# Deferred-norm FFN: one matmul of 512 columns for two of 256, with the sums of the parts taken on ScalarE and VectorE

## The chip, the core and the metric

The kernel runs on one core of a Trainium2 chip. The metric is the device time of one execution in microseconds (us); three runs of the kernel before give 2852.6 to 2856.93, median 2855.45.

## The reference

Two blocks of layers are computed one after the other on x of 256 tokens by 1,024 features. What matters here is the second block, which has four layers. Each does a mixer (differential attention, a gated linear recurrence, or a chunked gating unit), a cross attention to a memory, and then this FFN:

```python
def rmsnorm(x, g):
    y = xf * lax.rsqrt(jnp.mean(xf * xf, axis=-1, keepdims=True) + EPS)
    ...
def swiglu(h, w_gu, w_down):
    gate, up = jnp.split(h @ w_gu, 2, axis=-1)
    return (jax.nn.silu(gate) * up) @ w_down
...
        x = x + swiglu(rmsnorm(x, norm_ffn[i]), ffn_w_gu[i], ffn_w_down[i])
```

The inner width is 2,816. The first block has two layers with two FFNs each, with the same width, whose norm carries a modulation.

## The kernel before

**Precision.** Every large product is made from two parts: a value v is split into hi (v rounded to fp32r) and lo (v - hi), and three of the four products of parts are summed: weights hi x hi, weights hi x lo, weights lo x hi. The helper `product` (L1889 to L1891) issues these as three matmuls of 256 columns (the 256 tokens), each with a weight load of its own.

**Weights.** They stream from HBM through four slots in a fixed order. SyncE (queue SP) loads a unit into `raw`; ScalarE (ACT) rounds it to `whi` (L767); VectorE (DVE) forms `wlo` (L1187); TensorE (PE) uses both and signals `used`. A slot holds one unit, so its next split waits for `used`. The splits are issued by `ahead(pos)`, which stands between the other instructions of ACT and DVE and runs at most three units ahead. Both engines work in order, so a split waits behind whatever stands ahead of it.

**The FFN.** It has 11 steps of 256 inner features. Step n has a unit A (gate columns), a unit B (up columns) and two units O0, O1 (rows of the output weights). PE's order is A(0), B(0), then A(n+1), B(n+1), outs(n) for n from 0 to 9, and outs(10). A and B have each 16 groups (k, m): 8 tiles k of the features by two halves m of the 256 inner features. A is summed in the PSUM bank of its slot, both halves m in one bank; so is B. outs(n) has 48 matmuls (L2058; the last outs is L2091) into banks 4 to 7, from `ghi` and `glo`, the two parts of the product silu(A) x B.

**The deferred norm.** In the four FFNs of the second block (`st.defer` is set) x is not yet normalized when A and B are computed: `fhi`, `flo` (the halves of `parts_f`) are the parts of x times the gain, and the root of the norm, `rstd`, is multiplied in behind the matmuls. PE sums the squares (L2011) between A(0) and B(0); ACT takes Ln (L826) and Exp (L828) of that; DVE multiplies A by the root (L1381), ACT takes Silu (L853), DVE multiplies by the root again (L1384) and by B (L1389), ACT rounds to `ghi` (L866), DVE forms `glo` (L1393). In step 0 the split of A(1) stands behind Silu on ACT, and the split of B(1) behind `ghi`, which waits for the product. The FFNs of the first block go another way through the same functions (L858, L1400, L1403) and are not touched.

Of the kernel before, what the change touches and what calls it, by code (L numbers as in the profile page):

```python
# [29 lines left out]
P = 128  # L30
D = 1024
KT = D // P
# [202 lines left out]
def build(nc, a, out):  # L235

    ctx = ExitStack()
    with ctx:
# [51 lines left out]
        def work(at, *dims):  # L290
# [64 lines left out]
            "const_in const_rest mem_in token_in rows_first rows_in misc_in bias_out aux_in "  # L355
            "rows_turned misc_turned bias_mm vec_copied tok_turned tok_copied pro_v pro_s c_ready "
            "ada_sum ada_red ada_col "
            "ffn_out ffn_silu ffn_sr norm_sq norm_add norm_ss norm_ln norm_rs norm_gain norm_t norm_hi norm_lo "
            "ffn_hi ffn_lo ffn_scale x_new "
            "gn_sq gn_ss gn_ln gn_rs gn_out rope_mm rope_cos rope_done "  # L360
            "gate_mm gate_s gate_v taps_v conv_mm conv_v conv_s conv_hi conv_lo "
# [200 lines left out]
        def tiles4(v, cols, keep=slice(None)):  # L562
            return v.rearrange("p (c t) -> p c t", t=cols)[:, keep, :]

        def ffn_pos(st, j):

            base = st.pos + 2 + 4 * (j - 1)
            return (st.pos, st.pos + 1, None, None) if j == 0 else (base, base + 1, base + 2, base + 3)
# [11 lines left out]
        def summed(u):  # L580

            return 8 * (u if isinstance(u, int) and u <= ADA_BY_PE[0] else u - ADA_BY_PE[1] + ADA_BY_PE[0])

        SG_V = SG_T = 4
        MIX_F = (0, 20)

# [19 lines left out]
        def rows2(v):  # L606
            return v.rearrange("p (a b) -> p a b", a=2)
# [151 lines left out]
        def _(act):  # L759
# [85 lines left out]
            def ffn(st):  # L845
                A, B, _, O1 = st.slots
                lo0 = STEPS * st.i
                for j in range(STEPS):
                    pa, pb, o0, o1 = ffn_pos(st, j)
                    ahead(pa)  # L850
                    if st.defer is not None:
                        act.wait_ge(read[A], st.reads[A] + j + 1)
                        f(silu_a, silu_a, ACT.Silu).then_inc(q["ffn_silu"], 1)  # L853
                    else:
                        act.wait_ge(used[A], st.uses[A] + j + 1)
                        if st.reads[B] + j > 0:
                            act.wait_ge(read[B], st.reads[B] + j)
                        f(silu_a, ps[:, A, :], ACT.Silu).then_inc(read[A], 1)  # L858
                    ahead(pb)
                    if j:  # L860
                        ahead(o1, AHEAD if j < STEPS - 1 else 2)

                    act.wait_ge(read[B], st.reads[B] + j + 1)
                    if st.uses[O1] + j > 0:
                        act.wait_ge(used[O1], st.uses[O1] + j)
                    f(ghi[:, :, :], product, ACT.Copy).then_inc(q["ffn_hi"], 1)  # L866
                    if (st.i, j) == (0, 8):
                        rope_tables()
                    if (st.i, j) == (3, 1):
                        f(lam[:, 8:12], lam[:, 4:8], ACT.Exp).then_inc(q["c_ready"], 1)  # L870
                    if (st.i, j) == (3, 5):
                        act.wait_ge(*PRO.at(0, "mx_d"))
                        f(lb[:, 8:12, :], lb[:, 4:8, :], ACT.Exp).then_inc(q["c_ready"], 1)
                ahead(ffn_pos(st, STEPS)[3] - 2, 2)
# [301 lines left out]
        def _(dve):  # L1176
# [190 lines left out]
            def ffn(st):  # L1367
                lo0 = STEPS * st.i
                A, B, _, O1 = st.slots
                for j in range(STEPS):  # L1370
                    pa, pb, o0, o1 = ffn_pos(st, j)
                    ahead(pb if st.defer is None else pa)
                    if st.defer is not None:
                        n = STEPS * st.defer + j
                        dve.wait_ge(used[A], st.uses[A] + j + 1)
                        if j == 0:
                            dve.wait_ge(q["norm_rs"], st.late.i + 1)
                        if st.reads[B] + j > 0:
                            dve.wait_ge(read[B], st.reads[B] + j)
                        root = rstd[:, 1:2, :].broadcast_to([P, 2, S])  # L1380
                        tt(silu_a, rows2(ps[:, A, :]), root, ALU.mult).then_inc(read[A], 1)  # L1381
                        ahead(pb)
                        dve.wait_ge(q["ffn_silu"], n + 1)
                        tt(silu_a, silu_a, root, ALU.mult).then_inc(q["ffn_sr"], 1)  # L1384
                        dve.wait_ge(used[B], st.uses[B] + j + 1)
                        if lo0 + j > 0:
                            dve.wait_ge(q["ffn_lo"], lo0 + j)
                        dve.wait_ge(q["ffn_sr"], n + 1)
                        tt(product, rows2(ps[:, B, :]), silu_a, ALU.mult).then_inc(read[B], 1)  # L1389
                        ahead(o1 if j else pb + 1, AHEAD if j < STEPS - 1 else 2)  # L1390
                        dve.wait_ge(q["ffn_hi"], lo0 + j + 1)
                        dve.wait_ge(read[B], st.reads[B] + j + 1)
                        tt(glo[:, :, :], product, ghi[:, :, :].bitcast(F32), ALU.subtract).then_inc(q["ffn_lo"], 1)  # L1393
                        continue
                    dve.wait_ge(read[A], st.reads[A] + j + 1)
                    dve.wait_ge(used[B], st.uses[B] + j + 1)

                    if lo0 + j > 0:
                        dve.wait_ge(q["ffn_lo"], lo0 + j)
                    tt(product, silu_a, rows2(ps[:, B, :]), ALU.mult).then_inc(read[B], 1)  # L1400
                    ahead(o1 if j else pb + 1, AHEAD if j < STEPS - 1 else 2)
                    dve.wait_ge(q["ffn_hi"], lo0 + j + 1)
                    tt(glo[:, :, :], product, ghi[:, :, :].bitcast(F32), ALU.subtract).then_inc(q["ffn_lo"], 1)  # L1403
                    if st.ada and j < STEPS - 1:
                        u0, per = st.ada
                        for n in range(per[j] // 2):
                            ada_pair(u0 + sum(per[:j]) + 2 * n, n)
                    if (st.i, j) == (0, 4):
                        turned_angle("sin", turned_sin, 0.0)
                    if (st.i, j) == (0, 6):  # L1410
                        turned_angle("cos", turned_cos, 0.25)
                    if (st.i, j) == (3, 2):
                        lambdas()
                    if (st.i, j) == (3, 4):
                        bounds_spread()
                    if (st.i, j) == (3, 6):
                        lower_bounds()
# [457 lines left out]
        def _(pe):  # L1875
# [144 lines left out]
            def ffn(st):  # L2020
# [8 lines left out]
                def ab(slot, n, first=False):  # L2029

                    weights_of(slot, n)

                    if not (isinstance(n, int) and R[slot] + n == 0):
                        pe.wait_ge(read[slot], R[slot] + n)
                    th, tl = tiles(slot)
                    hi, lo = (hhi, hlo) if st.defer is None else (fhi, flo)
                    if first:
                        both(slot, th, tl, st.h, (hi, lo)).then_inc(used[slot], 1)
                        return
                    for m in range(2):  # L2040
                        for k in range(KT):
                            c = slice(P * m, P * m + P)
                            o = product(ps[:, slot, 256 * m:256 * m + 256], (th[:, k, c], tl[:, k, c]), hi[:, k, :],
                                        lo[:, k, :], k == 0, k == KT - 1)
                    o.then_inc(used[slot], 1)

                def outs(n, first=False):
# [11 lines left out]
                                       stop=False, skip_group_check=True)  # L2059
                        o.then_inc(used[slot], 1)  # L2060

                ab(A, 0, first=True)
                if st.defer is not None:
                    norm(st.late, True)
                ab(B, 0)

                def step(n, first=False):

                    ab(A, n + 1)
                    ab(B, n + 1)  # L2070
                    outs(n, first)

                u0, per = st.ada or (0, 10 * (0,))
# [387 lines left out]
```

## Time and profile before

| | |
|---|---|
| median of three runs | 2855.45 us |
| the profiled execution | 2852.6 us |
| its span | 2850.8 us |
| PE / weight load / DVE / ACT busy | 95% / 92% / 66% / 47% |
| mean granted clock of TensorE | 0.976 |
| matmuls in the trace | 22,439 |
| one step of a deferred FFN | 16.32 us |

The busy share of PE counts the time that any matmul is in flight, and matmuls overlap; the distance between the starts of two of them tells more. A wait that the profile can't put down to an instruction is called "issue".

### The profile page before, as it was taken

What the parts mean: (1) busy time and instruction counts of PE and PEld (TensorE: products, weight loads), DVE (VectorE), ACT (ScalarE), POOL (GpSimd) and SP (SyncE); (2) the same over time, 40 slices, a digit from 0 to 9 for tenths busy, and PEclk for the clock granted to TensorE, in tenths of its full rate; (3) what the DMA queues carried; (4) which work ended last, traced back from release to release, by engine and by line L of the source; (5) the groups of instructions that cost most, each with busy time, mean ns of one, the idle gap of its engine ahead of it and who ended that gap; (6) DMA issues with size and microseconds to landing.
All of it is one profiled execution on the core that took longest, in us unless ns stands there. A gap on an engine that the chain in (4) does not pass through costs nothing.

```text
span 2850.8 us, 53332 instructions
## 1 busy us (share of the span) xinstructions
PE 2707.0 (95%) x22439; PEld 2628.3 (92%) x22439; DVE 1890.2 (66%) x2639; ACT 1343.5 (47%) x1576; POOL 0.7 (0%) x5
## 2 busy tenths in 40 slices
PE   6799979999999799999999999999999999999998
PEld 6799959999999599999999999999999999999998
DVE  5877786877777855576565666656566555775564
ACT  3334634435446354465544535544465544555443
POOL 0000000000000000000000000000000000000000
PEclk8899979999999799999999999999999999999999
DMA  8988505997985045664355643535665266643552
GB/s 238 310 287 276 170 27 185 296 291 266 290 287 172 21 144 196 206 193 149 104 200 184 197 152 109 163 133 193 206 206 178 104 207 199 201 147 118 178 192 103
DMA packets 458802, 533.07 MB, mean 187 GB/s; under 512 B 9879, under 2 KB 435081, under 8 KB 458633
## 3 DMA queue, kind: packets, MB, share of 16 engines
q1 hardware_dynamic: 457340, 530.11, 56.9%
q8 instruction: 113, 1.85, 0.3%
q10 hardware_dynamic: 1293, 0.65, 0.1%
q14 instruction: 56, 0.46, 0.0%
HBM read 528.10 MB, written 2.62 MB: 186 GB/s over the span
## 4 chain that ended last, share of the span: by engine, by line
PE 79%; DVE 10%; DMA 3%; issue 3%; ACT 3%; SPq 1%; ACTq 0%; DVEq 0%
PE ps L2058 13%; PE ps L1889 11%; PE ps L1890 11%; PE ps L1891 11%; PE ps L1907 10%; PE ps L2426 8%; DMA work<-in_ada_w 3%; DVE work L1291 2%; DVE wlo L1187 2%; PE ps L2091 2%; DVE work L1563 2%; PE ps L2120 1%; PE ps L2236 1%; PE ps L2238 1%; PE ps L2237 1%
## 5 line engine op out<-in xcount | busy, mean ns | idle before, releaser
L1187 DVE TENSOR_TENSOR wlo<-raw,whi 128x2048 fp32r<-128x2048 f32 (+1 forms) x514 | 975.8, 1919 | 410.2 <-ACT whi L767 410.0
L767 ACT ACTIVATE whi<-raw 128x2048 fp32r<-128x2048 f32 (+1 forms) x514 | 826.4, 1615 | 436.5 <-PE ps L1891 148.0
L1889 PE MATMUL ps<-hhi,whi 128*128 128x256 f32 x1600 | 451.4, 282 | 13.8 <-issue 11.1
L1890 PE MATMUL ps<-hlo,whi 128*128 128x256 f32 x1600 | 445.0, 278 | 0.0
L1891 PE MATMUL ps<-hhi,wlo 128*128 128x256 f32 x1600 | 444.4, 278 | 0.0
L1889 PE MATMUL ps<-parts_f,whi 128*128 128x256 f32 x1344 | 372.6, 277 | 7.8 <-issue 7.8
L1890 PE MATMUL ps<-parts_f,whi 128*128 128x256 f32 x1344 | 371.5, 276 | 0.0
L1891 PE MATMUL ps<-parts_f,wlo 128*128 128x256 f32 x1344 | 371.2, 276 | 0.0
L2058 PE MATMUL ps<-ghi,whi 128*128 128x256 f32 x1280 | 355.5, 278 | 7.1 <-DVE wlo L1187 7.0
L2058 PE MATMUL ps<-glo,whi 128*128 128x256 f32 x1280 | 355.2, 278 | 0.0
L2058 PE MATMUL ps<-ghi,wlo 128*128 128x256 f32 x1280 | 354.9, 277 | 0.0
L1889 PEld LDWEIGHTS ps<-hhi,whi 128*128 128x128 f32 x1600 | 303.2, 190 | 18.0 <-issue 18.0
L1890 PEld LDWEIGHTS ps<-hlo,whi 128*128 128x128 f32 x1600 | 303.4, 190 | 0.7 <-issue 0.7
L1891 PEld LDWEIGHTS ps<-hhi,wlo 128*128 128x128 f32 x1600 | 302.9, 189 | 0.0
L1889 PEld LDWEIGHTS ps<-parts_f,whi 128*128 128x128 f32 x1344 | 252.3, 188 | 9.3 <-issue 9.2
L1890 PEld LDWEIGHTS ps<-parts_f,whi 128*128 128x128 f32 x1344 | 252.3, 188 | 0.1
L1891 PEld LDWEIGHTS ps<-parts_f,wlo 128*128 128x128 f32 x1344 | 252.3, 188 | 0.0
L2058 PEld LDWEIGHTS ps<-ghi,whi 128*128 128x128 f32 x1280 | 241.5, 189 | 8.2 <-issue 8.2
L2058 PEld LDWEIGHTS ps<-glo,whi 128*128 128x128 f32 x1280 | 241.5, 189 | 0.0
L2058 PEld LDWEIGHTS ps<-ghi,wlo 128*128 128x128 f32 x1280 | 241.4, 189 | 0.0
L1291 DVE SCALAR_TENSOR_TENSOR work<-work,silu_c 128x256 f32<-128x256 f32 x490 | 197.0, 479 | 0.0
L1907 PE MATMUL ps<-hhi,whi 128*128 128x256 f32 x880 | 177.5, 284 | 16.2 <-DVE hlo L1352 16.2
(277 smaller groups left out, 4892.0 us busy)
## 6 DMA issues: line engine op xcount, KB each, us to landing
raw<-in_ffn_w_in SPq DMA_DIRECT2D x88, 1024.0 KB, 10.6
raw<-in_ffn_w_gu SPq DMA_DIRECT2D x88, 1024.0 KB, 5.1
work<-in_ada_w SPq DMA_DIRECT2D x72, 1024.0 KB, 8.9
raw<-in_ffn_w_out SPq DMA_DIRECT2D x88, 512.0 KB, 6.0
raw<-in_ffn_w_down SPq DMA_DIRECT2D x88, 512.0 KB, 5.4
raw<-in_ca_w_kv SPq DMA_DIRECT2D x32, 1024.0 KB, 5.8
raw<-in_mix_w_in SPq DMA_DIRECT2D x24, 1024.0 KB, 6.3
raw<-in_da_w_in SPq DMA_DIRECT2D x24, 1024.0 KB, 6.0
```

Source lines behind the costliest of these rows:

```text
L767: f(whi[:, s, 0:size], raw[:, s, 0:size], ACT.Copy).then_inc(hi_done[s], 1)
L1187: tt(wlo[:, s, 0:size], raw[:, s, 0:size], whi[:, s, 0:size].bitcast(F32), ALU.subtract).then_inc(lo_done[s], 1)
L1291: m = stt(acc, w, silu_c[:, k:k + 1], acc, ALU.mult, ALU.add)
L1563: m = stt(conv_acc[:, t, :], h, w, conv_acc[:, t, :], ALU.mult, ALU.add)
L1889: mm(dst, wh, xh, start=first, stop=False)
L1890: mm(dst, wh, xl, start=False, stop=False)
L1891: return mm(dst, wl, xh, start=False, stop=last)
L1907: o = mm(ps[:, slot, 256 * m:256 * m + 256], w[:, k, P * m:P * m + P], x_[:, k, :], start=k == 0 and i == 0 and m == 0, stop=k == KT - 1 a ...
L2058: o = mm(dst, a_, b_[:, t, :], start=first and t == 0 and i == 0 and m % 2 == 0, stop=False, skip_group_check=True)
L2091: o = mm(dst, a_, b_[:, t, :], start=False, stop=t == 1 and i == 2 and m % 2 == 1, skip_group_check=True)
L2120: o = mm(d[:, c], K[rows_, tile, c], Q[rows_, tile, c], start=True, stop=True)
L2426: o = mm(ps[:, bank, 256 * m:256 * m + 256], w[:, k, P * m:P * m + P], x_[:, k, :], start=k == 0 and i == 0 and m == 0, stop=k == KT - 1 a ...
```

## The change

In the deferred FFNs, `product` is replaced for A and B. Per (k, m) one matmul of 512 columns multiplies weights hi with [fhi | flo] side by side and fills a whole bank; a second one of 256 columns adds weights lo x fhi into the left half. A takes two banks now (A's and B's), B the other two (O0's and O1's). The two halves of a bank are summed outside PE: ACT copies the right halves to the work buffer (new semaphores `wide_a`, `wide_b`) and DVE adds the left ones. DVE's multiply by the root and by B then work on the sum, with semaphores of their own (`ffn_a`, `ffn_prod`). The bank is free after the addition instead of after the multiply. A(0) and B(0) wait for two banks each.

```diff
+        def wide_banks(st):
+
+            A, B, O0, O1 = st.slots
+            return tuple(slice(min(n, m), max(n, m) + 1, abs(n - m)) for n, m in ((A, B), (O0, O1)))
+
+        TILE_ORDER = [(k, m) for m in range(2) for k in range(KT)]
+        FIRST_ORDER = [(k, m) for k in range(KT) for m in range(2)]
...
                     if st.defer is not None:
-                        act.wait_ge(read[A], st.reads[A] + j + 1)
+                        banks_a, banks_b = wide_banks(st)
+                        n = STEPS * st.defer + j
+                        act.wait_ge(used[A], st.uses[A] + j + 1)
+                        if n:
+                            act.wait_ge(q["ffn_prod"], n)
+                        f(silu_a, ps[:, banks_a, S:], ACT.Copy).then_inc(q["wide_a"], 1)
+                        act.wait_ge(q["ffn_a"], n + 1)
                         f(silu_a, silu_a, ACT.Silu).then_inc(q["ffn_silu"], 1)
...
                     ahead(pb)
+                    if st.defer is not None:
+                        act.wait_ge(used[B], st.uses[B] + j + 1)
+                        act.wait_ge(q["ffn_lo"], lo0 + j)
+                        f(product, ps[:, banks_b, S:], ACT.Copy).then_inc(q["wide_b"], 1)
                     if j:
                         ahead(o1, AHEAD if j < STEPS - 1 else 2)
 
                     act.wait_ge(read[B], st.reads[B] + j + 1)
+                    if st.defer is not None:
+                        act.wait_ge(q["ffn_prod"], STEPS * st.defer + j + 1)
...
                     if st.defer is not None:
-                        n = STEPS * st.defer + j
+                        banks_a, banks_b = wide_banks(st)
                         dve.wait_ge(used[A], st.uses[A] + j + 1)
                         if j == 0:
                             dve.wait_ge(q["norm_rs"], st.late.i + 1)
-                        if st.reads[B] + j > 0:
-                            dve.wait_ge(read[B], st.reads[B] + j)
+                        n = STEPS * st.defer + j
+                        if n:
+                            dve.wait_ge(q["ffn_prod"], n)
                         root = rstd[:, 1:2, :].broadcast_to([P, 2, S])
-                        tt(silu_a, rows2(ps[:, A, :]), root, ALU.mult).then_inc(read[A], 1)
+                        dve.wait_ge(q["wide_a"], n + 1)
+                        tt(silu_a, ps[:, banks_a, 0:S], silu_a, ALU.add).then_inc(read[A], 1)
+                        dve.wait_ge(read[A], st.reads[A] + j + 1)
+                        tt(silu_a, silu_a, root, ALU.mult).then_inc(q["ffn_a"], 1)
                         ahead(pb)
                         dve.wait_ge(q["ffn_silu"], n + 1)
                         tt(silu_a, silu_a, root, ALU.mult).then_inc(q["ffn_sr"], 1)
-                        dve.wait_ge(used[B], st.uses[B] + j + 1)
-                        if lo0 + j > 0:
-                            dve.wait_ge(q["ffn_lo"], lo0 + j)
+                        dve.wait_ge(q["wide_b"], n + 1)
+                        tt(product, ps[:, banks_b, 0:S], product, ALU.add).then_inc(read[B], 1)
+                        dve.wait_ge(read[B], st.reads[B] + j + 1)
                         dve.wait_ge(q["ffn_sr"], n + 1)
-                        tt(product, rows2(ps[:, B, :]), silu_a, ALU.mult).then_inc(read[B], 1)
+                        tt(product, product, silu_a, ALU.mult).then_inc(q["ffn_prod"], 1)
...
+                def ab_wide(slot, n, banks, first=False):
+
+                    weights_of(slot, n)
+                    if first:
+                        for b in banks:
+                            pe.wait_ge(read[b], R[b])
+                    else:
+                        pe.wait_ge(read[slot], R[slot] + n)
+                    th, tl = tiles(slot)
+                    for k, m in FIRST_ORDER if first and slot == A else TILE_ORDER:
+                        if first and slot == A and m == 0:
+                            pe.wait_ge(q["norm_lo"], 8 * st.h + k + 1)
+                        c = slice(P * m, P * m + P)
+                        mm(ps[:, banks[m], :], th[:, k, c], parts_f[:, :, k, :], start=k == 0, stop=False)
+                        o = mm(ps[:, banks[m], 0:S], tl[:, k, c], fhi[:, k, :], start=False, stop=k == KT - 1)
                     o.then_inc(used[slot], 1)
...
-                ab(A, 0, first=True)
                 if st.defer is not None:
+                    ab_wide(A, 0, sorted((A, B)), first=True)
                     norm(st.late, True)
-                ab(B, 0)
+                    ab_wide(B, 0, sorted((O0, O1)), first=True)
+                else:
+                    ab(A, 0, first=True)
+                    ab(B, 0)
...
-                    ab(A, n + 1)
-                    ab(B, n + 1)
+                    if st.defer is not None:
+                        ab_wide(A, n + 1, sorted((A, B)))
+                        ab_wide(B, n + 1, sorted((O0, O1)))
```

## Rows read from the trace of the kernel before

**Rows 1.** The page: busy time by engine, and the chain that ended last.

```profile
PE 2707.0 (95%) x22439; PEld 2628.3 (92%) x22439; DVE 1890.2 (66%) x2639; ACT 1343.5 (47%) x1576; POOL 0.7 (0%) x5
...
PE 79%; DVE 10%; DMA 3%; issue 3%; ACT 3%; SPq 1%; ACTq 0%; DVEq 0%
```

**Rows 2.** Window totals, nine steps of the first deferred FFN: busy us, clock, DMA.

```profile
core 0: us, PE busy (x) PEld busy (x) DVE busy (x) ACT busy (x) POOL busy (x), PEclk, DMA share, GB/s
...
1453.97:1600.86 146.89, 146.89 (x1299) 146.89 (x1298) 88.15 (x74) 62.32 (x55) 0.00 (x0) 1.00 0.59 197
```

**Rows 3.** Timeline from 1499.94: start us, duration us, engine, line, tiles.

```profile
1499.94 0.28 PE L1891 MATMUL ps<-parts_f,wlo 128*128 128x256 f32 x1
1499.94 0.19 PEld L1889 LDWEIGHTS ps<-parts_f,whi 128*128 128x128 f32 x1
...
1500.28 0.28 PE L1891 MATMUL ps<-parts_f,wlo 128*128 128x256 f32 x1
```

**Rows 4.** The chain, start of the first deferred FFN: start us, us, what.

```profile
1434.03 0.86 PE ps L2011 x4
...
1440.38 1.65 issue
1442.04 0.35 PE ps L1889
...
1447.73 0.53 issue
1448.26 0.36 PE ps L1889
...
1453.97 5.44 PE ps L2058 x48
```

**Rows 5.** Timeline of DVE there; in brackets the idle time and its releaser.

```profile
1435.94 0.69 DVE L1381 TENSOR_TENSOR work<-ps,rstd 128x512 f32<-128x512 f32 x1 [2.88 <-ACT rstd L828]
...
1441.85 0.68 DVE L1384 TENSOR_TENSOR work<-work,rstd 128x512 f32<-128x512 f32 x1
1442.67 0.69 DVE L1389 TENSOR_TENSOR work<-ps,work 128x512 f32<-128x512 f32 x1
...
1450.35 0.68 DVE L1393 TENSOR_TENSOR glo<-work,ghi 128x512 fp32r<-128x512 f32 x1
1450.95 0.68 DVE L1381 TENSOR_TENSOR work<-ps,rstd 128x512 f32<-128x512 f32 x1
```

**Rows 6.** Timeline of ACT there.

```profile
1435.44 0.42 ACT L828 ACTIVATE rstd<-rstd 128x256 f32<-128x256 f32 x1
1435.87 1.28 ACT L853 ACT_TABLE_LOAD   x1
1437.17 0.63 ACT L853 ACTIVATE work<-work 128x512 f32<-128x512 f32 x1
```

**Rows 7.** Timeline of DVE and ACT at the end of the same FFN.

```profile
1600.89 0.69 DVE L1389 TENSOR_TENSOR work<-ps,work 128x512 f32<-128x512 f32 x1 [1.27 <-PE ps L1891]
...
1606.39 0.63 ACT L866 ACTIVATE ghi<-work 128x512 fp32r<-128x512 f32 x1 [4.38 <-PE ps L2058]
```

**Rows 8.** The chain, other stretches: one-column and plain 512-column matmuls.

```profile
52.16 0.80 PE ps L1949 x8
...
1275.60 0.86 PE ps L2106 x2
```

**Rows 9.** ACT's groups by shape: copies out of PSUM, busy us and mean ns.

```profile
L909 ACT ACTIVATE work<-ps 128x512 f32<-128x512 f32 x84 | 49.9, 594 | 145.7 <-PE ps L1907 66.9 <-PE ps L1891 37.6 <-PE ps L2238 27.9
```

**Rows 10.** Timeline of DVE in a later step of that FFN: splits.

```profile
1517.05 2.29 DVE L1187 TENSOR_TENSOR wlo<-raw,whi 128x2048 fp32r<-128x2048 f32 x1 [2.51 <-ACT whi L767]
...
1520.08 0.69 DVE L1389 TENSOR_TENSOR work<-ps,work 128x512 f32<-128x512 f32 x1
1521.30 3.43 DVE L1187 TENSOR_TENSOR wlo<-raw,whi 128x2048 fp32r<-128x2048 f32 x2 [0.53 <-ACT whi L767]
```

**Rows 11.** Window totals of two stretches of 8 us elsewhere.

```profile
452.00:460.00 8.00, 5.18 (x26) 4.71 (x25) 5.31 (x14) 4.18 (x9) 0.00 (x0) 0.79 0.00 0
...
1674.00:1682.00 8.00, 5.93 (x39) 5.76 (x38) 6.59 (x12) 0.00 (x0) 0.00 (x0) 0.79 0.41 131
```

More of the change, by code:

```diff
@@ L357, in build @@
             "ada_sum ada_red ada_col "
-            "ffn_out ffn_silu ffn_sr norm_sq norm_add norm_ss norm_ln norm_rs norm_gain norm_t norm_hi norm_lo "
+            "ffn_out wide_a wide_b ffn_a ffn_silu ffn_sr ffn_prod norm_sq norm_add norm_ss norm_ln norm_rs norm_gain norm_t norm_hi norm_lo "
             "ffn_hi ffn_lo ffn_scale x_new "
@@ L1384, in ffn @@
                         tt(silu_a, silu_a, root, ALU.mult).then_inc(q["ffn_sr"], 1)
-                        dve.wait_ge(used[B], st.uses[B] + j + 1)
-                        if lo0 + j > 0:
-                            dve.wait_ge(q["ffn_lo"], lo0 + j)
+                        dve.wait_ge(q["wide_b"], n + 1)
+                        tt(product, ps[:, banks_b, 0:S], product, ALU.add).then_inc(read[B], 1)
+                        dve.wait_ge(read[B], st.reads[B] + j + 1)
                         dve.wait_ge(q["ffn_sr"], n + 1)
-                        tt(product, rows2(ps[:, B, :]), silu_a, ALU.mult).then_inc(read[B], 1)
+                        tt(product, product, silu_a, ALU.mult).then_inc(q["ffn_prod"], 1)
                         ahead(o1 if j else pb + 1, AHEAD if j < STEPS - 1 else 2)
                         dve.wait_ge(q["ffn_hi"], lo0 + j + 1)
-                        dve.wait_ge(read[B], st.reads[B] + j + 1)
+                        dve.wait_ge(q["ffn_prod"], n + 1)
                         tt(glo[:, :, :], product, ghi[:, :, :].bitcast(F32), ALU.subtract).then_inc(q["ffn_lo"], 1)
@@ L2035, in ab @@
                     th, tl = tiles(slot)
-                    hi, lo = (hhi, hlo) if st.defer is None else (fhi, flo)
                     if first:
-                        both(slot, th, tl, st.h, (hi, lo)).then_inc(used[slot], 1)
+                        both(slot, th, tl, st.h).then_inc(used[slot], 1)
                         return
@@ L2042, in ab @@
                             c = slice(P * m, P * m + P)
-                            o = product(ps[:, slot, 256 * m:256 * m + 256], (th[:, k, c], tl[:, k, c]), hi[:, k, :],
-                                        lo[:, k, :], k == 0, k == KT - 1)
+                            o = product(ps[:, slot, 256 * m:256 * m + 256], (th[:, k, c], tl[:, k, c]), hhi[:, k, :],
+                                        hlo[:, k, :], k == 0, k == KT - 1)
+                    o.then_inc(used[slot], 1)
+                def ab_wide(slot, n, banks, first=False):
[12 more added lines that the diff above has]
+                        o = mm(ps[:, banks[m], 0:S], tl[:, k, c], fhi[:, k, :], start=False, stop=k == KT - 1)
                     o.then_inc(used[slot], 1)
@@ L2060, in outs @@
                         o.then_inc(used[slot], 1)
-                ab(A, 0, first=True)
                 if st.defer is not None:
+                    ab_wide(A, 0, sorted((A, B)), first=True)
                     norm(st.late, True)
-                ab(B, 0)
+                    ab_wide(B, 0, sorted((O0, O1)), first=True)
+                else:
+                    ab(A, 0, first=True)
+                    ab(B, 0)
                 def step(n, first=False):
-                    ab(A, n + 1)
-                    ab(B, n + 1)
+                    if st.defer is not None:
+                        ab_wide(A, n + 1, sorted((A, B)))
+                        ab_wide(B, n + 1, sorted((O0, O1)))
+                    else:
+                        ab(A, n + 1)
+                        ab(B, n + 1)
                     outs(n, first)
```

## The prediction

> **What bounds the kernel now.** I read the page first. TensorE (PE) is busy for 95% of the span and holds 79% of the chain that ended last [rows 1], but matmuls overlap in that count, so next come the window totals and the matmul starts. The diff touches only the four FFNs whose norm is deferred, the last of which ends near the end of the span. Over nine whole steps of the first of them, from one group of output matmuls to the tenth, PE is busy for 146.89 of 146.89 us at clock 1.00 [rows 2]: 16.32 us a step, for 144 matmuls (48 each for A, B and the outputs), or 113.3 ns a matmul. The single starts say the same: 1499.94 to 1500.28 is three matmuls, 340 ns [rows 3]. In that stretch VectorE (DVE) works 88.15/9 = 9.8 us a step and ScalarE (ACT) 62.32/9 = 6.9 us; neither sets the pace. PE does wait at three places of every such FFN. The chain of waits shows 1.65 us of "issue" ahead of A(1) and 0.53 us ahead of B(1) [rows 4]; the timelines of DVE and ACT [rows 5, 6] show that these are waits for the split of the weights, which stands in the in-order queues behind the elementwise work of step 0. The third is at the end, where the last glo waits for outs(9) [rows 7]. The other three deferred FFNs repeat the pattern (1.4 to 1.7 us and 0.3 to 0.5 us).
>
> **Matmuls: what is removed.** For each (k, m), three matmuls of 256 columns with three weight loads become one of 512 columns (weights hi against [x hi | x lo]) and one of 256 (weights lo against x hi): the columns are the same 768, and one load and one matmul fewer. Units: 11 steps x 2 x 4 FFNs = 88, each of 16 groups, so 1,408 matmuls and loads go. What a group gains depends on what makes up the 113.3 ns. 256 columns at 2.4 GHz are 106.7 ns. Eight one-column matmuls, each with its own 128-column load, take 0.80 us, 100 ns apiece [rows 8], so a load alone nearly fills a slot. Plain fp32 matmuls have twice the array time: the 256-column ones take 0.86/4 = 215 ns [rows 4], the 512-column ones, recorded in two parts, 0.86/2 = 430 ns a part [rows 8]. That is 213.3 and 426.7 ns of columns plus 2 to 3 ns: with the load hidden under the stream, nearly nothing is added. So I take the 512-column slot at 216 ns and leave the 256-column one at 113.3, as the next load is still only covered by 256 columns: 329.3 against 340, a gain of g = 10.7 ns a group. Bounds: the wide slot at 2 x 113.3 = 226.6 gives g = 0; both slots at pure column time (213.3 + 106.7) give g = 20. The value chosen is the nearer to a row, that of the 215 ns slots.
>
> The weight load of each matmul starts with the matmul ahead of it, on the same rows of the array, and both repeat every 113 ns [rows 3]: loads are hidden under matmuls today. The Trainium skill (page "TensorE: Matmul & The Clock Gate", "Measured speedup vs the span model", on what overlaps) says that a weight load runs beside a matmul in flight only when their row groups differ; the trace disagrees here, and by the rule a slot would be over 200 ns and a removed load worth its whole length. The same page ("Back-to-back issue gap") gives the Trainium skill's sustained 131 ns for 512 columns; by it, as an estimate, a group would gain 96 ns, which no row bears out.
>
> **Where that gain counts.** Of a deferred FFN's 22 units, A(0) (16 groups), B(1) and the 18 units of the later steps lie on the path. B(0) and A(1) don't: what follows each is waiting for elementwise work (below), so what they save is only waited longer. That is 20 x 16 = 320 groups, 320 x 10.7 ns = 3.42 us an FFN.
>
> **Elementwise work: what is added.** Per step two ACT copies out of PSUM (a 512-element one takes 594 ns [rows 9]) and two DVE additions (0.69 us as L1381 and L1389 [rows 5]). A's sum is divided over copy, add, multiply by root; B's over copy, add, multiply. In the steady steps they are covered. The low part of A's next weights is ready at 1517.05 + 2.29 = 1519.34 [rows 10] and is due when outs ends, at 1524.70 (1453.97 + 4 x 16.32 + 5.44 [rows 4]): 5.4 us of slack, of which copy and dependent add take about 1.5. The next product, now 1520.08 + 0.69 [rows 10], moves some 2.2 us back; behind it on DVE are B's and O0's splits, 3.43 us from 1521.30 [rows 10], done by 1527 instead of 1524.7 and due after 1530. DVE goes to 11.2 us and ACT to 8.1 us of a step of 16.32 - 32 x 0.0107 = 15.98 us. If that cover were gone, each step could cost up to the 0.59 + 0.82 us of a copy and an add, 1.4 us x 36 = 50 us; DVE would have to be over 4 us later for that.
>
> The bank waits don't bite. A now fills two banks and B the other two, but each pair is read out and refilled in the order of before, and its copy and add end some 1.5 us after the unit, while the refill is 10 us off. The two new banks at the start were read by the output projection before the norm was made.
>
> At the end of the FFN the last product is made at 1600.89 + 0.69, and ghi waits until 1606.39 for outs(9) [rows 7]. Copy, add and the dependent multiply add 1.5 us: covered, 0.
>
> **Step 0 is not covered.** Chain now: Exp ends at 1435.86 [rows 6], L1381 (x root) 1435.94 to 1436.63 [rows 5], the Silu table 1435.87 to 1437.15, Silu at 1437.17 [rows 6], A(1)'s split high and low, PE at 1442.04 [rows 4]. After: the copy stands between Exp and the table load, 1435.86 to 1436.45; add from 1436.53 to 1437.22; the multiply needs its result, and dependent DVE operations start 0.82 us apart (1441.85 to 1442.67 [rows 5]), so 1437.35 to 1438.04; the table load is over by then; Silu at 1438.08. That is 0.91 us later, and with it A(1). Then silu x root, the add for B right behind it (independent DVE operations are 0.60 apart, 1450.35 to 1450.95 [rows 5]), and the multiply 0.82 behind that: 0.60 more. ghi, B(1)'s split (queued behind ghi on ACT) and B(1) are 0.91 + 0.60 = 1.51 us late. A(2) is next: its low part, ready near 1456.4 now, moves back by 1.51 and another 0.8, to 1458.7, while PE comes to it at 1453.97 + 5.44 + 1.2 = 1460.6. It is covered, and the steps from there run free.
>
> So an FFN gains 3.42 - 1.51 = 1.91 us; four gain 7.6 us.
>
> **Clock.** The idle time ahead of A(1) grows from 1.65 by 0.91 and by the 0.17 that B(0) saves, to 2.7 us. In the stretches from 452 and from 1674 us, with 2.8 and 2.1 us of idle PE, the granted clock is 0.79 over 8 us [rows 11], which is 3.4 us at the lower level, 1.7 us lost. Such a fall here would lie in A(1), behind which PE now waits 0.53 + 0.60 + 0.17 = 1.3 us, so some 0.4 us of it would show. I count two of four: +0.8 us.
>
> Sum: -7.6 + 0.8 = -6.8 us. The profiled execution took 2852.6 us with a span of 2850.8, so it would be 2845.8; it was the fastest of the three runs, whose median is 2855.45, and from that I forecast 2848.6.
>
> **Rivals.**
> 1. *The slot goes by columns, so nothing is gained* (g = 0 to 2). The load of 100 ns speaks against it, that no 512-column matmul of this data type is in the trace speaks for it. What is left is the later start: 4 x 1.51 = +6.0 us, +0.8 for the clock: 2862, slower. It decides where g falls below 1.51/320 = 4.7 ns.
> 2. *Gain and cost nearly cancel*: the wide slot keeps the 6.6 ns over column time (220, g = 6.7), or the start costs twice what I have: -2.5 or -1.6 us, 2853 to 2854.
> 3. *Both slots fall to column time plus 2 ns* (216 and 109, g = 15): 320 x 15 - 1510 = 3.3 us an FFN, -13 us, 2842. Against it: with 100 ns, one load fits under 256 columns already, and yet the slot is 113.
> 4. *DVE's or ACT's order breaks the cover* in the steady steps (a copy that waits behind a split, the split due next): place is the low part of A(n+2) ahead of its unit; it decides when that is over 5.4 us later than now, and each further 0.2 us a step costs 36 x 0.2 = 7 us: around 2860.
> 5. *A load is not hidden today*: removing one of 100 ns [rows 8] would give 320 x 0.1 x 4 = 128 us, 2727. Loads and matmuls that both repeat every 113 ns [rows 3] nearly exclude it. (This is what the rule of the Trainium skill's page "TensorE: Matmul & The Clock Gate" above would bring.)
>
> **How the numbers follow.** Forecast 0.62; rival 1 0.08; rival 2 0.17; rival 3 0.06; rival 4 0.06; rival 5 0.01. Measurement tells 0.2% (5.7 us) from no change. The forecast's 6.8 us is barely beyond that, with 1.5 us to either side from how well copy and add times are known and how often the clock falls, so three quarters of it are faster and the rest the same. Faster 0.62 x 0.77 + 0.07 = 0.55; same 0.14 + 0.16 = 0.30; slower 0.15. Range: the likeliest case by itself is 2846 to 2851; down to 2842 it takes in rival 3, up to 2858 rival 2 and part of 1 and 4.
>
> **What would show it.** Right: starts of a 512-column matmul and the next 216 ns apart, then 113; steps of 15.98 us with PE busy throughout; the wait ahead of A(1) 2.7 us and ahead of B(1) 1.3 us; Silu of step 0 2.2 us after the end of Exp, its table load under DVE's work; the 1.5 us ahead of the last outputs unchanged. Wrong: a slot of 226 (rival 1), idle PE inside the loop (rival 4), a table load ahead of the copy, which would put A(1) another 1.3 us later, or waits at B(0) for banks.

## The result: slower by 0.7%, and the profile after

The changed kernel takes 2876.26 us (median of 4 runs, 2873.92 to 2881.87) against 2856.19 us before (median of 4): ratio 1.0073, 95% interval 1.0057 to 1.0089. I had forecast 2848.6 us and a range of 2842 to 2858. The profiled execution took 2870.35 us with a span of 2868.6 us, 17.8 us more than before. The medians differ by 20.1 us; the 2 us more weren't traced.

The page of the changed kernel: busy time by engine, the chain that ended last, and two of its groups.

```profile
PE 2717.4 (95%) x21031; PEld 2579.0 (90%) x21031; DVE 1940.6 (68%) x2727; ACT 1389.5 (48%) x1664; POOL 0.7 (0%) x5
...
PE 83%; DVE 9%; ACT 3%; issue 3%; DMA 2%; SPq 1%; ACTq 0%; DVEq 0%
...
L2082 PE MATMUL ps<-parts_f,whi 128*128 128x512 f32 x1408 | 497.7, 396 | 11.9 <-issue 11.9
...
L2083 PE MATMUL ps<-parts_f,wlo 128*128 128x256 f32 x1408 | 396.2, 281 | 0.0
```

The 1,408 matmuls are gone (22,439 to 21,031), and yet PE's share of the chain rose from 79% to 83% [rows 1]. Next the window totals, nine steps of the first and of the second deferred FFN.

```profile
1455.29:1606.13 150.84, 150.84 (x1009) 138.15 (x1008) 97.72 (x92) 73.11 (x73) 0.00 (x0) 1.00 0.57 192
1914.99:2063.90 148.91, 148.91 (x1010) 137.00 (x1009) 96.83 (x91) 72.86 (x73) 0.00 (x0) 1.00 0.57 195
```

PE is still busy throughout at full clock, and a step takes 16.76 us in the first and 16.55 in the second, where it took 16.32 [rows 2] and I expected 15.98. So no wait has come in; the matmuls themselves are slower. Their starts, in the timeline of the first FFN, show it:

```profile
1500.05 0.40 PE L2082 MATMUL ps<-parts_f,whi 128*128 128x512 f32 x1
1500.28 0.28 PE L2083 MATMUL ps<-parts_f,wlo 128*128 128x256 f32 x1
1500.40 0.40 PE L2082 MATMUL ps<-parts_f,whi 128*128 128x512 f32 x1
```

I call the time from the start of a matmul to the start of the next its slot (the four places for weights are the weight slots). A wide matmul (512 columns) has a slot of 233 ns and a narrow one (256) of 120, together 353 instead of the 340 of three matmuls [rows 3]. In the second and fourth FFN they are 229 and 117.6, together 347. Between the first matmul of A(0) and the last of the FFN, the four take 190.50, 188.88, 190.50 and 188.38 us; before it was 184.86, 185.05, 184.86 and 185.05. The sum of the differences is 18.4 us, all of the 17.8 and a little more. Of it, about 12 us are the longer steps (nine steps take 3.95 us more in two of the FFNs and 2.02 in the other two); the remaining 6.4 us lie at the start, where the later start of A(1) and B(1) and the longer slots of its own units add up.

The chain at the start of the first FFN:

```profile
1434.53 0.86 PE ps L2034 x4
...
1441.05 2.25 issue
1443.29 0.47 PE ps L2082
...
1449.18 0.89 issue
1450.07 0.47 PE ps L2082
...
1455.94 5.47 PE ps L2097 x48
```

and what ACT does there:

```profile
1435.94 0.42 ACT L835 ACTIVATE rstd<-rstd 128x256 f32<-128x256 f32 x1
1436.27 0.58 ACT L864 ACTIVATE work<-ps 128x512 f32<-128x512 f32 x1
1436.86 1.28 ACT L866 ACT_TABLE_LOAD   x1
1438.43 0.63 ACT L866 ACTIVATE work<-work 128x512 f32<-128x512 f32 x1 [0.28 <-DVE work L1404]
```

Counted from the norm's matmul, A(1) starts 8.76 us later instead of 8.01 and B(1) 15.54 instead of 14.23 [rows 4]: 0.75 and 1.31 us more. The copy (L864) stands between Exp and the table load, and Silu waits for DVE, not for the table.

### The profile page after: what moved, and what is told of

The parts are those of the page before. It is cut to its first block, busy times and chain, and to the rows that moved or that the text cites. A ratio compares the mean times of both kernels' runs of the same rounds, so it can differ in the third digit from the quotient of the medians.

```text
span 2868.6 us, 50786 instructions
## 1 busy us (share of the span) xinstructions
PE 2717.4 (95%) x21031; PEld 2579.0 (90%) x21031; DVE 1940.6 (68%) x2727; ACT 1389.5 (48%) x1664; POOL 0.7 (0%) x5
## 4 chain that ended last, share of the span: by engine, by line
PE 83%; DVE 9%; ACT 3%; issue 3%; DMA 2%; SPq 1%; ACTq 0%; DVEq 0%
PE ps L2097 14%; PE ps L2082 11%; PE ps L1930 9%; PE ps L2472 7%; PE ps L1912 7%; PE ps L1913 6%; PE ps L1914 6%; PE ps L2083 6%; DVE wlo L1206 2%; PE ps L2137 2%; DMA work<-in_ada_w 2%; DVE work L1586 2%; PE ps L2166 1%; PE ps L2282 1%; PE ps L2284 1%
## 5 line engine op out<-in xcount | busy, mean ns | idle before, releaser
L2082 PE MATMUL ps<-parts_f,whi 128*128 128x512 f32 x1408 | 497.7, 396 | 11.9 <-issue 11.9
L1913 PE MATMUL ps<-hlo,whi 128*128 128x256 f32 x1600 | 445.2, 278 | 0.0
L1914 PE MATMUL ps<-hhi,wlo 128*128 128x256 f32 x1600 | 444.7, 278 | 0.0
L2083 PE MATMUL ps<-parts_f,wlo 128*128 128x256 f32 x1408 | 396.2, 281 | 0.0
L2082 PEld LDWEIGHTS ps<-parts_f,whi 128*128 128x128 f32 x1408 | 266.0, 189 | 72.5 <-issue 13.9
L2083 PEld LDWEIGHTS ps<-parts_f,wlo 128*128 128x128 f32 x1408 | 265.9, 189 | 0.1
L1930 PE MATMUL ps<-hlo,whi 128*128 128x256 f32 x880 | 174.5, 280 | 0.0
L1930 PE MATMUL ps<-hhi,wlo 128*128 128x256 f32 x880 | 174.0, 280 | 0.0
```

The lines of the kernel that those rows point to most:

```text
L2082: mm(ps[:, banks[m], :], th[:, k, c], parts_f[:, :, k, :], start=k == 0, stop=False)
L2083: o = mm(ps[:, banks[m], 0:S], tl[:, k, c], fhi[:, k, :], start=False, stop=k == KT - 1)
```

## Experiments

Ten kernels were run: seven variants of the two kernels, and three that time streams of matmuls by themselves.

### x1: two matmuls of 256 columns for the wide one

```diff
-                        mm(ps[:, banks[m], :], th[:, k, c], parts_f[:, :, k, :], start=k == 0, stop=False)
+                        mm(ps[:, banks[m], 0:S], th[:, k, c], fhi[:, k, :], start=k == 0, stop=False, ...)
+                        mm(ps[:, banks[m], S:], th[:, k, c], flo[:, k, :], start=False, stop=False, ...)
...
```

> The changed kernel with each 512-column matmul cut into two of 256 columns (hi into the left half of the bank, lo into the right half), everything else kept: two banks a unit, the copies and the additions. Theory A (the wide matmul's slot alone costs the steps their time): slots go back to 113 ns and a step to 16.32 us; what is left against the kernel before is the later start of A(1) and B(1), about 1.3 us an FFN, so +5 us in all (ratio 1.002), or +7 with a fall of the clock. Theory B (copies out of PSUM, additions or the second bank slow TensorE's writes): the slots stay above 113 and the step stays near 16.76 and 16.55 us, +18 to +20 us.

Measured: ratio 1.0023 (1.0008 to 1.0037). The chain of x1_split:

```profile
1435.45 2.41 issue
...
1443.56 1.08 issue
...
1450.35 5.44 PE ps L2098 x48
1466.67 5.44 PE ps L2098 x48
```

The step is back at 16.32 us, and what stays is the start (FFNs of 186.2 to 186.9 us, 1.3 to 1.9 above before, 6.6 us in all four). Theory A holds: copies, additions and second banks cost the steps nothing; the wide matmul alone makes them longer.

### x2: first the wide matmuls of a half, then the narrow ones

```diff
...
+                        for m in range(2):
+                            c = slice(P * m, P * m + P)
+                            for k in range(KT):
+                                mm(ps[:, banks[m], :], th[:, k, c], parts_f[:, :, k, :], start=k == 0, stop=False)
+                            for k in range(KT):
+                                o = mm(ps[:, banks[m], 0:S], tl[:, k, c], fhi[:, k, :], start=False, stop=k == KT - 1)
...
```

> The changed kernel with the order of a unit's matmuls changed (all units but A(0)): for each half, first the 8 wide matmuls, then the 8 narrow ones. Theory A1 (512 columns of fp32r cost 226 ns or more of themselves): wide to wide is 226 to 234 ns, narrow to narrow 113, a step 16.3 to 16.6 us. Theory A2 (a wide slot is 216 ns and the alternation of wide and narrow adds the rest, the load of the one being read while the other streams): wide to wide 216, narrow to narrow 113, a step 15.98 us, some 3 us an FFN faster than the changed kernel's 16.76.

Measured: ratio 1.0059 (1.0042 to 1.0076). Wide to wide is 226 to 236 ns, mean 233 in the first FFN and 228 in the second; narrow to narrow 116 to 122, mean 118, in the first and 113 to 119, mean 114, in the second. Steps are 16.91 us in the first FFN and 16.43 in the second. The 216 ns of theory A2 appear nowhere, so it isn't the alternation. Two sizes fell outside both expectations: the step of the first FFN grew, and its output matmuls, which nobody touched and whose buffers all stand where they stood, went from 5.47 us in the changed kernel to 5.71:

```profile
1452.52 5.71 PE ps L2106 x48
```

### x3: the two parts side by side in SBUF

```diff
-        parts_f = sb("parts_f", [P, 2, KT, S], F32R)
-        fhi, flo = parts_f[:, 0], parts_f[:, 1]
+        parts_f = sb("parts_f", [P, KT, 2, S], F32R)
+        fhi, flo = parts_f[:, :, 0, :], parts_f[:, :, 1, :]
...
-                        mm(ps[:, banks[m], :], th[:, k, c], parts_f[:, :, k, :], start=k == 0, stop=False)
+                        mm(ps[:, banks[m], :], th[:, k, c], parts_f[:, k].rearrange("p t s -> p (t s)"), start=k == 0, stop=False)
```

> The changed kernel with the two parts of a tile side by side, so that the wide matmul reads 512 neighbouring columns instead of two runs of 256 that lie 8 KB apart. Theory P (the second run costs the time): the wide slot falls from 229 to 234 ns to 216 and a step to about 16 us. Theory A1 (the columns cost it, wherever they lie): 229 to 234 ns as before. Theory D (the place of the operands in SBUF against the weights matters): slots of another size, not 216, and different for the FFNs as before.

Measured: ratio 1.0059 (1.0036 to 1.0082), steps 16.76 and 16.55 us, wide slots 229 to 234 ns. The two separate runs of 256 columns cost nothing; theory P falls.

### m1: TensorE alone

The kernel fills the operands, runs streams of 32 groups and copies x to the output; it leaves the whole computation out.

> TensorE alone, all other engines idle, on operands at the addresses of the kernel; it computes nothing of the reference (the output is a copy of x). Streams of 32 groups each: the three-matmul form and the wide-and-narrow form with the weights in each of the four slots, the same with neighbouring columns, wide only, narrow only, wides then narrows, and the wide-and-narrow form with the moving operand shifted by 4 to 56 elements. Theory A1: the wide slot is 226 or more in all of them. Theory P: 216 where the columns are neighbours, 229 and more where not. Theory D: slots change with the weight slot and the shift, between 216 and 236, and the three-matmul form too, between 109 and 120. If other engines are to blame (theory B), all streams here are at 216 and 113.

The chain of m1_streams, start, us and number of matmuls. L83 to L93 are the three-matmul form with weights in weight slots 1, 2 and 3, L98 to L108 wide and narrow with weight slots 0 to 2 (3 is as 2), L118 and L123 the same with neighbouring columns (weight slots 0 and 2), L128 wide only, L138 256 columns only, L144 and L146 eight wide and then eight narrow.

```profile
48.89 11.41 PE ps L83 x96
60.31 10.88 PE ps L88 x96
71.19 10.88 PE ps L93 x96
82.07 11.09 PE ps L98 x64
93.16 11.10 PE ps L103 x64
104.25 11.30 PE ps L108 x64
...
126.86 11.10 PE ps L118 x64
137.96 11.30 PE ps L123 x64
149.26 7.34 PE ps L128 x32
...
163.92 3.77 PE ps L138 x32
167.69 1.85 PE ps L144 x8
169.53 0.91 PE ps L146 x8
```

Divided by 32 groups: the three-matmul form takes 357 ns in weight slot 1 (and in 0, once that stream, the first, has left its slow start) and 340 in 2 and 3; the wide form 347 in 0 and 1 and 353 in 2 and 3, side by side or not; a wide matmul by itself 229 and one of 256 columns 118, but 114 in a batch of eight behind eight wide ones. With every other engine idle the wide form has the numbers of the kernel: A and B stand in weight slots 2 and 3 in the first and third FFN (353) and in 0 and 1 in the second and fourth (347). The three-matmul form doesn't carry over so simply: it runs at 340 ns in the second and fourth FFN as well, with weights in 0 and 1, where the stream takes 357. Theory B is out, A1 holds (the wide slots are 225 ns and more everywhere), and the place of the operands goes with the rest, as theory D has it.

Twelve more streams of m1 shift the moving operand, a second buffer at the same place modulo 256 bytes as parts_f, with weights in weight slot 0. The wide form takes 347 to 353 ns at eight shifts; the three-matmul form 340, 355, 340 and 357 at shifts of 0, 16, 32 and 48 elements. So at shift 0 it runs at 340, and on parts_f, at the same place modulo 256, at 357: that place alone doesn't set its pace.

### m2: columns, weight columns, data type

The streams run one matmul per group; the output is again a copy of x.

> TensorE alone again (the output is a copy of x). Streams of 32 matmuls of fp32r with 512, 448, 384, 320 and 256 columns and 128 weight columns, with 64 and 32 weight columns, bf16 with 512 and 256 columns, and one with the same weights and moving tile throughout. Theory R (fp32r columns stream slower than one per clock, whatever is loaded): the slot grows by 0.44 to 0.46 ns a column and fewer weight columns change nothing, 226 and more at 512. Theory L (each weight load takes from the stream, as both read SBUF): the slope is 0.417 ns a column, a constant of 13 to 20 ns stands on it, and it shrinks with 64 and 32 weight columns, to 216 ns at 512. bf16 is 216 and 109 in both.

The chain of m2_lengths, 32 matmuls a line: fp32r with 448 and 256 columns (L87, L99; 384 and 320 between them took 5.59 and 4.69 us); 512 and 256 columns with 64 weight columns (L103, L107) and with 32 (L111, L115); bf16 with 512 and 256 columns (L119, L123).

```profile
50.95 6.47 PE ps L87 x32
...
67.70 3.77 PE ps L99 x32
71.47 7.40 PE ps L103 x32
78.86 3.81 PE ps L107 x32
82.67 7.42 PE ps L111 x32
90.09 3.73 PE ps L115 x32
93.83 6.92 PE ps L119 x32
100.75 3.49 PE ps L123 x32
```

From 256 to 448 columns the slot grows from 117.8 to 202.2 ns: 0.44 ns a column, where 2.4 GHz would give 0.417, and about 5 ns stand on it. The first stream (512 columns, 128 weight columns) starts at 427 ns a slot, half the pace, though the clock row of the profile shows no fall there; its second half runs at 233. So 128, 64 and 32 weight columns give 233, 231 and 232 ns, while the recorded load shrinks from 188 to 135 and 109 ns. The last stream (L126, 7.47 us), with one weight tile and one moving tile throughout, is at 233 as well. bf16 takes 216 and 109 ns. So it is theory R: at full clock fp32r operands stream slower than one column per clock, and the weight load has next to no part in it. All these streams stand at one kind of place; the 0.44 and the 5 ns are those of that place.

### x4: parts_f moved to a place 128 bytes off modulo 256

```diff
+        parts_f = sb("parts_f", [P, 2, KT, S], F32R)
         sb("phase_m", [P, 32])
...
-        parts_f = sb("parts_f", [P, 2, KT, S], F32R)
```

The edit does more than that: mhi, mlo, ghi and glo, the output matmuls' operands among them, move up by the 16 KB of parts_f. That keeps their place modulo 256 bytes, not their address.

> The changed kernel with parts_f allocated 128 bytes off its place modulo 256 (ahead of a pad and of mhi, instead of behind glo); all other buffers keep theirs. In the streams the wide and narrow slots are 229 and 117 ns with weights in slots 0 and 1, and 233 and 120 in slots 2 and 3, whose place is 128 bytes off, and the four FFNs have A and B in slots 2, 3 (first, third) and 0, 1 (second, fourth). Theory D (the place of the moving operand against that of the weights sets this part): the FFNs change roles, steps near 16.55 us in the first and third and near 16.76 in the second and fourth; in all no change (18 us above the kernel before). Theory S (the slot numbers, or what else those FFNs have in them, set it): the steps stay 16.76 and 16.55 where they were.

Measured: ratio 1.0090 (1.0074 to 1.0105), above the changed kernel's 1.0073, with intervals that overlap; in the profiles the four FFNs take 5.7 us more than the changed kernel's. The chain of x4_phase, output matmuls of the first FFN, then of the second:

```profile
1476.25 5.71 PE ps L2097 x48
1493.04 5.71 PE ps L2097 x48
```

```profile
1936.77 5.44 PE ps L2097 x48
```

The groups of A and B did change roles: 346.5 ns in the first FFN, 353.4 in the second. But the first FFN's step is 16.79 us all the same, because its output matmuls now take 118.9 ns a slot instead of 113.9. Whether the matmuls ahead of them or the 16 KB do that, x4 doesn't tell; x2 has the same 118.9 with no buffer moved. In the third FFN the first step took 16.55 us, with output matmuls at 113.8 ns, and all later ones 16.79, at 118.9: both paces at the same addresses. So the place of parts_f matters (theory D for the groups), and what ran before matters too; "no change in all" was wrong.

### m3: is there a place where the wide form wins?

> TensorE alone (the output is a copy of x). Streams of 32 groups, weights in slot 2, the moving operand shifted by 0, 4, ... 60 elements; first 16 streams in the wide-and-narrow form, then 16 in the three-matmul form. If 226 + 113 ns is within reach at some place, the wide form could at best draw level with the 340 ns of the three-matmul form; if fp32r's 0.44 ns a column with some 5 ns a matmul held for both, the wide form would be at 344 and the other at 354 wherever the other misses its 113 ns. I expect the three-matmul form at 113 to 114 ns a slot at every eighth shift or so (16 bytes a step of the pattern unknown) and 118 to 119 at the others, and the wide form between 345 and 353 ns at all of them, so that it never gains on 340.

The chain of m3_places: second and fourteenth place of the wide form, then first, second, sixth and eleventh of the three-matmul form (32 groups a line, 64 or 96 matmuls).

```profile
48.10 11.23 PE ps L85 x64
...
182.11 11.37 PE ps L157 x64
...
215.86 10.92 PE ps L175 x96
226.78 11.42 PE ps L181 x96
...
272.30 10.96 PE ps L205 x96
...
328.84 11.60 PE ps L235 x96
```

From the starts in the second half of each stream: the wide form takes 347 to 356 ns a group at all 16 places (the first stream starts at half the pace, as in m2). The three-matmul form takes 340 at shifts 0 and 20 and 353 to 363 at the other fourteen. As expected the wide form never reaches 340; but at 13 of the 14 places where the three-matmul form misses 340 the wide form is faster, by 3 to 13 ns. That the shifts with 340 would come every eighth was wrong, there are two.

Weight slot 2 (m3) lies 128 bytes off weight slot 0 (m1) modulo 256, so the shifted streams of the two runs can be paired by the place of the moving operand against the weights. The wide form has the same pace within 0.2 ns in six of eight pairs, between 346.6 and 353.4 ns, with another stream ahead; in two it hasn't (346.6 and 346.7 against 350.0). The three-matmul form agrees in three of four (340, 355, 357); in the fourth it is at 340.0 in m1 and at 356.7 in m3. Each place was timed once and in one order, so what else decides isn't separated.

### The start: A(1)'s split ahead of the norm chain

```diff
                 if st.early or st.defer is not None:
                     ahead(st.pos)
+                if st.defer is not None:
+                    ahead(st.pos + 1, 1)
...
                     add_up(st)
                     ahead(st.pos)
+                    ahead(st.pos + 1, 1)
                     return
```

On the kernel before:

> The kernel before, with the split of A(1) in a deferred FFN issued ahead of the norm's Ln on ScalarE and ahead of the multiply by the root on VectorE, instead of behind Silu. If the two waits at the start of these FFNs are what I read them to be (A(1)'s split queued behind the norm chain, B(1)'s behind the product), A(1) follows B(0) at once, B(1) follows A(1) with no wait or a short one, and each FFN is up to 2.2 us shorter (1.65 + 0.53): -6 to -8 us, ratio 0.9973 to 0.998. If something else holds A(1) (its transfer, say), no change.

Measured: ratio 0.9969 (0.9958 to 0.9981), 2845.86 us against 2854.23. ACT in v_before_early:

```profile
1437.09 1.91 ACT L767 ACTIVATE whi<-raw 128x2048 fp32r<-128x2048 f32 x1 [3.38 <-PE ps L1910]
1438.91 0.46 ACT L828 ACTIVATE rstd<-ps,con 128x256 f32<-128x256 f32 x1
```

and its chain:

```profile
1436.99 0.86 PE ps L2014 x4
...
1448.79 0.26 issue
1449.05 0.36 PE ps L1892
```

The split now runs ahead of Ln, the 1.65 us of wait ahead of A(1) are gone, and B(1) starts 12.06 us behind the norm's matmul instead of 14.23. The four FFNs are 2.2, 2.0, 2.2 and 2.0 us shorter: 8.4 us, and the medians of the runs differ by 8.4 us too.

On the changed kernel:

> The changed kernel with the same earlier split of A(1). The slots stay as they are (step 16.76 and 16.55 us), and the waits ahead of A(1) and B(1), 2.5 and 1.2 us, go or shrink: -10 to -14 us against the changed kernel, so +4 to +9 us against the kernel before, which is what the slots alone cost (20 units x 16 groups x 7 to 13 ns an FFN is 2.2 to 4.2 us, 13 in all, less the shorter start).

Measured: ratio 1.0022 (1.0011 to 1.0033), 6.6 us above the kernel before. A(1) follows at once; the wait ahead of B(1) did not shrink but is 1.39 us in the chain, where the changed kernel has 0.89. Steps are 16.76 and 16.55 us. FFNs of 188.5 and 186.5 us are 3.7 and 1.5 longer than before: the slower slots, partly paid by the better start. The four together are 10.4 us longer, more than the runs give (3 to 9 us); that difference wasn't traced. Against the changed kernel the ratios (1.0073 and 1.0022) give 14.6 us less and the profiled FFNs 8.1, where 10 to 14 were expected.

Last, on the kernel before again, with the high part of B(1)'s split moved ahead of ghi as well:

```diff
...
                     if j:
                         ahead(o1, AHEAD if j < STEPS - 1 else 2)
+                    elif st.defer is not None:
+                        ahead(pb + 1)
```

> The kernel before with the earlier split of A(1), and ScalarE's part of the split of B(1) moved ahead of its wait for the product as well. The wait ahead of B(1), 0.54 and 0.20 us with the first move alone, should fall to 0.11 (one slot): each FFN another 0.1 to 0.4 us shorter, about 1 us in all and too little to be told by the runs (ratio 0.996 to 0.998). If ghi, now behind three splits on ScalarE, is late for outs(0), a wait appears there instead and the gain is gone.

Measured: ratio 0.9961 (0.9947 to 0.9976), 2842.55 us against 2855.06. No wait is left ahead of B(1) (0.11 to 0.12 us from slot to slot), and the first and third FFN are 0.5 us shorter still, at 182.18 us; the second is 0.15 longer, the fourth 0.1 shorter. Against v_before_early that is within what the runs can tell. It beats both kernels of this case.

## Why the prediction was wrong, point by point

**The wide slot at 216 ns: this step failed, and with it the sign.** I took the 512-column slot from plain fp32 matmuls. The x4 of L2011 [rows 4] are two matmuls recorded in two parts each (the kernel issues two there), and a part takes 215 ns for 256 columns: two clocks a column, 213.3 ns, and 2 more. The eight one-column records of rows 8 are likewise four matmuls, so the 100 ns were those of a part, and of plain fp32. I read the 6.6 ns that an fp32r slot has over its columns as the weight load's doing, because that load is nearly as long. m2 shows that the load has next to no part in it and that the excess grows with the columns (11 ns over column time at 256, 15.5 at 448, some 20 at 512). What I needed was a row of fp32r with another length; there was none, and I let the nearest row of another kind decide instead of the bound of 2 x 113.3 = 226.6. That bound was itself too low: the slot is 229 to 233.

**The narrow slot at 113.3: wrong too.** It became 117 to 120. The 113.3 ns are one of the paces of a 256-column matmul and not a constant: streams of it alone take 117 to 119 (m1, m2), batches of eight behind wide ones 114 (m1, the second FFN of x2) or 118 (the first FFN of x2). The three-matmul form has 113.3 at 4 of 8 streams of m1 and at 2 of 16 places of m3, and in all four FFNs of the kernel before, so the change gave up more than the matmul it saved. A group costs 353.3 or 346.7 ns against the 329.3 forecast; over 320 groups an FFN that is 7.7 and 5.6 us more than I had, 26.5 us in all four. From the forecast -7.6 to the measured +18.4 it is 26.0 us, so this one term is nearly the whole error.

**Which units count:** right. B(0) and A(1) are followed by waits in the changed kernel too, save A(1) of the second FFN, which the fall of the clock (below) made longer.

**Elementwise work covered in the steps:** right, shown by x1 (16.32 us a step with all of it in place). DVE does 10.9 and ACT 8.1 us a step.

**The start:** mechanism right, size near: counted from the norm's matmul, A(1) is 0.75 us late for 0.91 forecast and B(1) 1.31 for 1.51. Dependent DVE operations were 0.72 us apart there, not 0.82, and the copy overlapped Exp by 0.09.

**The clock:** in the profile the fall came in one FFN of four, in A(1) of the second, as these window totals show.

```profile
1900.00:1908.00 8.00, 5.65 (x23) 4.64 (x22) 5.18 (x5) 4.26 (x6) 0.00 (x0) 0.79 0.40 131
1903.45:1906.20 2.75, 2.75 (x10) 2.36 (x9) 0.97 (x2) 1.66 (x2) 0.00 (x0) 0.50 0.90 295
```

That FFN took 188.88 us and the fourth, without a fall, 188.38: 0.5 us, where I had 0.4. Its A(1) lasted 7.25 us and B(1) followed without a wait, so the rest was indeed covered. The second line holds a clue: at 0.50 of the clock, the lower level of 1.2 GHz, a wide and a narrow matmul together take 640 ns, 0.833 ns for each of 768 columns. That is one column per clock with nothing on it. What fp32r takes over its columns shows at full clock alone.

**The rivals:** rival 1 had the right place (the columns set the slot) and g = 0 as its bound; what happened is g = -7 and -13, outside the range. That g could be negative I hadn't considered.

**The page on weight loads:** the sentence that the prediction draws on stands under "The mechanism" of the Trainium skill's page "TensorE: Matmul & The Clock Gate", not under the section named there. m2 disagrees with it as rows 3 do: loads recorded at 188 ns repeat every 118 ns beside the matmuls.

What stays open is why the same matmuls take 113 ns at some places and after some predecessors, and 118 at others. The place of the operands (the wide form in m1, m3 and x4) and what ran before (x2, the third FFN of x4) both move it; I have no mechanism that is shown.

## What to carry to other kernels

Before matmuls are merged or split, time one stream of exactly that data type and length, because a slot read from another type can hide a cost that grows with the columns; a small kernel with PE alone gave in one run the wide form's numbers, which decided this case. The old form must be timed in its kernel as well: alone it ran at 357 ns where the kernel has 340. Where a kernel already runs at the shortest slot seen, any change to the sequence can lose that state, also in neighbouring matmuls that are not touched. And when a profile shows a wait that an in-order queue causes (here a split behind a norm chain), moving the queued work is the cheaper change: it gave 8 to 12.5 us where the new matmul form cost 20.

## What the runs showed of the hardware that I had not expected

- fp32r matmuls stream at 0.44 ns a column at full clock (117.8 ns at 256, 202.2 at 448 columns), bf16 at one column per clock (109 and 216 ns at 256 and 512). At the lower level fp32r too takes one column per clock (640 ns for 768 columns at a granted clock of 0.50, in the changed kernel). The Trainium skill (page "TensorE: Matmul & The Clock Gate", "Back-to-back issue gap") gives N/2.4 + 2.5 ns for the gap of a single warm matmul without a word on the type: bf16 agrees here, fp32r at 512 columns is 10 to 20 ns above it. The Trainium skill's sustained 131 ns for 512 columns isn't borne out by any stream here.
- The number of weight columns (128, 64, 32) changes the slot of an fp32r matmul by 2 ns at most (233, 231, 232 ns at 512 columns; 118, 119, 117 at 256).
- The same sequence of fp32r matmuls has more than one steady pace (340 or 353 to 363 ns for three of 256 columns). For the wide form it goes mostly with the place of the moving operand against the weights modulo 256 bytes (six of eight pairs of streams agree within 0.2 ns). What ran before counts as well: output matmuls went from 113.9 to 118.9 ns a slot when only the order of the matmuls ahead of them was changed (x2).
